# Hybrid encoder trunk: in the state-space groups, D times input moves to ScalarE, the masks come from the table of all heads, Y stands ahead of the last convolution, the scaling is shared and the chunk halves alternate

## The chip, the cores and the metric

The program runs on one core of one Trainium2 chip. The metric is device time in microseconds (us), the median of a few executions. TensorE (PE in the profile) multiplies matrices, VectorE (DVE), ScalarE (ACT) and GpSimd (POOL) do the elementwise work, and SyncE (SP) starts the loads of weights. The engines run side by side and wait for each other only by semaphores.

## The reference, cut to what matters

One layer over 512 frames and 1024 channels: a feed-forward part, a mixer of three branches (gated linear attention, a Mamba-2 state-space branch, chunked attention), another feed-forward part. The change touches the state-space branch alone:

```python
def _ssd(xh, bm, cm, dt, a):            # per chunk of 64 frames
        cum = jnp.cumsum(dac, axis=1)
        seg = cum[:, :, None] - cum[:, None, :]
        decay = jnp.exp(jnp.where(mask, seg, -jnp.inf))
        cb = jnp.einsum('btgn,bsgn->btsg', cc, bc)
        xdt = xc * dtc[..., None]
        y = jnp.einsum('btsg,btsgr,bsgrp->btgrp', cb, decay, xdt)
        y = y + jnp.einsum('btgn,bgrpn->btgrp', cc, state) * jnp.exp(cum)[..., None]
        to_end = jnp.exp(cum[:, -1:] - cum)
        state = jnp.exp(cum[:, -1])[..., None, None] * state + jnp.einsum('bsgn,bsgrp->bgrpn', bc, xdt * to_end[..., None])
...
    y = _ssd(xh, bm, cm, dt, a) + ssm_D.astype(F32).reshape(SSM_GROUPS, SSM_HPG)[..., None] * xh
    y = y.reshape(bsz, seq, SSM_D_INNER) * jax.nn.silu(z.astype(F32))
    y = _rmsnorm(y.reshape(bsz, seq, SSM_GROUPS, SSM_D_INNER // SSM_GROUPS), ...)
```

There are 8 groups of 4 heads of 64 channels, and 8 chunks of 64 frames. x, B and C come out of a projection, a causal convolution over 4 frames and a SiLU.

## The kernel before

Weights come from memory as 297 slabs of 128x1024, in the order of their use, into a ring of three buffers (RAW). ScalarE rounds each slab to WH (`hi`, L1025), VectorE subtracts to get the rest WL (`lo`, L1443), and TensorE multiplies WH by both parts of the activations and WL by one. So each slab costs three passes of eight matmuls (L534, and L576 for the z projection), and a slab must have been split before TensorE can use it. Every engine has its own program in a fixed order written by hand; the only thing that binds them is the semaphores.

The state-space groups take the time from about 427 us to 787 us. One pass of the loop (`ssm_round`) does two things at once: it projects and convolves the group p = i + 1, and carries out the chunked scan of the group `inner` = i, whose convolved x, B and C lie ready. In TensorE's order, a pass is:

- projection slab n (24 matmuls), then `ssm_turn`: twelve transposes of x into I01 and of B into I2, and the four `seg` matmuls (L677, L678) into I34, from the masked decay table MSH and its rest MSL
- slab n+1, then `ssm_cb_u`: the product C times B per chunk (L684), and seven state updates (L690, L695) from BK and XTE, whose results overwrite I01 and I34
- slabs n+2 and n+3, then `ssm_inter` (L712) and `ssm_intra` (L704: 32 small products of M and XDT, 64x64 each)
- the z projection of slabs n+4 and n+5 (L576, 96 matmuls), then `turn_back` (L721): eight transposes of Y.

Around it, ScalarE starts each convolution (L1109), copies I01 to XD (L1132) and I2 to BK, takes the exponential of I34 as M, the tanh of each convolution (L1120), the squares of Y (L1142), and evicts the turned Y (L1152). VectorE does the taps of the convolutions (L1626, three each), the SiLU products (L1645), XDT and XTE = XD times a factor for each head (L1665, L1667), the mask of CB, the chain of the states (13 steps), Y in four steps (L1705 to L1713), the variance (L1718), the scaling of Y (L1721), and MSH (L1609). GpSimd does MSL (L433), XD times D (L444) and the power -1/2 (L446). The first group has a prologue (`ssm_first`); the last one runs without a next group, beside the merge of this branch's output.

A few names: `gsc` is a copy of the 4 columns of a group out of SC, the table of all 32 heads. I01, I2, I34 and G are the banks of PSUM. Each matmul of f32 operands that isn't fp32r stands in the profile as two, so `ssm_intra` has 64 rows in the trace, and L684 has 16.

```python
                inc(nc.scalar.copy(XD[:].rearrange("p j c -> p (j c)"), I01[:]), "x_copied")
...
                x4 = XD[:].rearrange("p j (r c) -> p j r c", r=HPG)
                inc(nc.gpsimd.tensor_tensor(x4, x4, d, ALU.mult), "xd_ready")
```

Of the kernel before, what the change touches and what calls it, by code (L numbers as in the profile page):

```python
# [19 lines left out]
ALU = mybir.AluOpType  # L20
# [57 lines left out]
class At:  # L78
# [27 lines left out]
    def read(self):  # L106
# [9 lines left out]
        "ssm_squares": 4, "ssm_hi": 2,  # L116
# [5 lines left out]
        "m_ready": 1, "conv_done": 4, "ssm_chain": 13, "ssm_y": 4, "ssm_var": 1, "ssm_scaled": 4, "ssm_lo": 2,  # L122
# [4 lines left out]
    "gpsimd": {"da_lo_masked": 1, "xd_ready": 1, "ssm_rstd": 1, "gla_rstd": 1},  # L127
# [20 lines left out]
def build(nc, a, out):  # L148

    ctx = ExitStack()  # L150
    with ctx:
# [24 lines left out]
        minus_half = sb("minus_half", [P, TT])  # L176

# [176 lines left out]

        def over_tiles(ap):

            return ap.unsqueeze(1).to_broadcast([P, TT, HS])
# [39 lines left out]
        def _(pool):  # L397
# [11 lines left out]
            link(nc.gpsimd.memset(minus_half[:], -0.5))  # L409
            link(nc.gpsimd.memset(wgk_raw, 0.0))  # L410
# [18 lines left out]
            def da_lo(g):  # L429

                pool.wait_ge(sems["group_const"], after("group_const", g))
                pool.wait_ge(sems["intra_done"], last("intra_done", g - 1))
                inc(nc.gpsimd.tensor_tensor(MSL[:].rearrange("p (q t) -> p q t", t=CH),  # L433
                                            bc(gsc[:, 28:32, :].rearrange("p j r -> p (j r)"), CH),
                                            causal[:].unsqueeze(1).to_broadcast([P, TT * HPG, CH]), ALU.mult),
                    "da_lo_masked")

            def ssm(g):

                pool.wait_ge(sems["xte_ready"], after("xte_ready", g))  # L440
                pool.wait_ge(sems["group_norm"], after("group_norm", g))
                d = ggrp[:, 2:6].unsqueeze(1).unsqueeze(3).to_broadcast([P, TT, HPG, CH])
                x4 = XD[:].rearrange("p j (r c) -> p j r c", r=HPG)
                inc(nc.gpsimd.tensor_tensor(x4, x4, d, ALU.mult), "xd_ready")  # L444
# [54 lines left out]
            with pool.Fori(0, NG) as i:  # L499
                da_lo(i)  # L500
                ssm(i)

# [18 lines left out]
        def _(pe):  # L521
# [159 lines left out]
            def ssm_cb_u(g):  # L681
# [5 lines left out]
                pe.wait_ge(sems["xte_ready"], after("xte_ready", g))  # L687
                pe.wait_ge(sems["x_copied"], after("x_copied", g))
# [1472 lines left out]
```

## Time and profile before

| what | value |
|---|---|
| median of 3 executions | 1847.29 us (1846.70 to 1848.17) |
| the profiled execution's own time | 1847.36 us |
| its span in the trace | 1845.5 us |
| granted clock of TensorE, mean | 0.995 |
| busy: PE, DVE, ACT, POOL | 98%, 53%, 33%, 8% |

The profiled execution took what the others took, and its span leaves out 1.9 us at the ends. The busy share of PE counts every matmul from its start to its modelled end, and matmuls overlap; where TensorE really waits is seen from the idle time before its instructions, which the trace gives with the instruction that released them.

### The profile page before, as it was taken

The numbers are of one execution on the slowest core, as the hardware profiler recorded it, in microseconds if no ns is written. First come the engines' busy times: TensorE is split into PE (matmuls) and PEld (weight loads), VectorE is DVE, ScalarE is ACT, GpSimd is POOL, SyncE is SP. The second block draws the span as 40 slices with busy tenths as digits, with TensorE's granted clock in tenths as the row PEclk, the third lists the DMA queues.
The fourth block names the chain that finished last, engine by engine and source line by source line (L and its number), as shares of the span: only waits on it lengthen the run. The fifth ranks groups of instructions, "written<-read, shape, count | busy, mean of one in ns | idle before, by whom it ended". The sixth has DMA issues, their size and how long they took to land.

```text
span 1845.5 us, 26225 instructions
## 1 busy us (share of the span) xinstructions
PE 1806.9 (98%) x9852; PEld 1508.4 (82%) x9852; DVE 977.6 (53%) x1376; ACT 610.7 (33%) x942; POOL 145.1 (8%) x116
## 2 busy tenths in 40 slices
PE   7999999999999999999999999999999999999997
PEld 5888888878888888788988888887888888888885
DVE  6444443379888888732444445545334544444333
ACT  4323222233333344332233334443222422323221
POOL 4111100031111111100000000000000011111000
PEclk9999999999999999999999999999999999999998
DMA  4323223322222222132222222222222322223331
GB/s 154 103 93 100 93 101 103 110 84 70 73 74 69 68 68 68 58 103 91 92 69 82 90 87 82 84 78 89 95 99 91 103 92 92 101 92 101 103 105 66
DMA packets 47352, 164.91 MB, mean 89 GB/s; under 512 B 5520, under 2 KB 6672, under 8 KB 47296
## 3 DMA queue, kind: packets, MB, share of 16 engines
q1 hardware_dynamic: 43584, 158.10, 26.1%
q10 hardware_dynamic: 3712, 6.03, 1.0%
q8 instruction: 39, 0.64, 0.1%
q14 instruction: 17, 0.14, 0.0%
HBM read 162.01 MB, written 2.10 MB: 89 GB/s over the span
## 4 chain that ended last, share of the span: by engine, by line
PE 70%; issue 21%; DVE 6%; POOL 1%; ACT 1%; DMA 0%; DVEq 0%; POOLq 0%; ACTq 0%; SPq 0%
PE G L534 33%; PE G L576 12%; PE I L534 9%; PE G L550 7%; DVE WL L1443 2%; DVE CV L1626 1%; PE I L896 1%; POOL hid L456 1%; PE I L930 1%; PE I L906 1%; PE I L704 1%; PE I L712 1%; PE G L761 1%; DVE UL L1459 1%; DVE un L1581 1%
## 5 line engine op out<-in xcount | busy, mean ns | idle before, releaser
L1443 DVE TENSOR_TENSOR WL<-RAW,WH 128x1024 fp32r<-128x1024 f32 x297 | 387.9, 1309 | 298.2 <-ACT WH L1025 290.2
L1025 ACT CAST WH<-RAW 128x1024 fp32r<-128x1024 f32 x297 | 309.6, 1048 | 230.9 <-PE I L534 126.2
L534 PE MATMUL G<-UH,WH 128*128 128x512 f32 x696 | 172.8, 390 | 0.0
L534 PE MATMUL G<-UH,WL 128*128 128x512 f32 x696 | 171.9, 389 | 0.0
L534 PE MATMUL G<-UL,WH 128*128 128x512 f32 x696 | 171.9, 389 | 0.0
L534 PEld LDWEIGHTS G<-UH,WH 128*128 128x128 f32 x696 | 130.6, 188 | 28.0 <-issue 1.0
L534 PEld LDWEIGHTS G<-UH,WL 128*128 128x128 f32 x696 | 130.6, 188 | 27.1
L534 PEld LDWEIGHTS G<-UL,WH 128*128 128x128 f32 x696 | 130.6, 188 | 27.1
L534 PE MATMUL G<-NH,WH 128*128 128x512 f32 x448 | 113.2, 395 | 1.4 <-ACT SC L1098 1.4
L534 PE MATMUL G<-NL,WH 128*128 128x512 f32 x448 | 110.7, 389 | 0.0
L534 PE MATMUL G<-NH,WL 128*128 128x512 f32 x448 | 110.6, 389 | 0.0
L534 PEld LDWEIGHTS G<-NH,WH 128*128 128x128 f32 x448 | 82.4, 188 | 21.6 <-issue 5.1
L534 PEld LDWEIGHTS G<-NL,WH 128*128 128x128 f32 x448 | 84.1, 188 | 17.6
L534 PEld LDWEIGHTS G<-NH,WL 128*128 128x128 f32 x448 | 84.1, 188 | 17.5
L576 PE MATMUL G<-WH,NH 128*128 128x256 f32 x640 | 91.7, 286 | 3.6 <-DVE WL L1443 3.6
L576 PE MATMUL G<-WL,NH 128*128 128x256 f32 x640 | 91.0, 285 | 0.0
L576 PE MATMUL G<-WH,NL 128*128 128x256 f32 x640 | 90.7, 285 | 0.0
L456 POOL TENSOR_TENSOR hid<-hid,rms 128x512 f32<-128x512 f32 x44 | 57.3, 1302 | 397.8 <-ACT hid L1059 397.8
L576 PEld LDWEIGHTS G<-WH,NH 128*128 128x128 f32 x640 | 83.0, 192 | 6.2 <-issue 5.0
L534 PE MATMUL I<-HH,WH 128*128 128x512 f32 x352 | 87.6, 389 | 0.0
L534 PE MATMUL I<-HL,WH 128*128 128x512 f32 x352 | 87.6, 389 | 0.0
L534 PE MATMUL I<-HH,WL 128*128 128x512 f32 x352 | 87.6, 389 | 0.0
(299 smaller groups left out, 2477.5 us busy)
## 6 DMA issues: line engine op xcount, KB each, us to landing
RAW<-in_slabs SPq DMA_DIRECT2D x297, 512.0 KB, 3.3
h<-in_x SPq DMA_DIRECT2D x4, 512.0 KB, 6.8
bias<-in_rel ACTq DMA_DIRECT2D x16, 128.0 KB, 3.0
out_y<-h ACTq DMA_DIRECT2D x8, 256.0 KB, 2.2
bias<-in_rel ACTq DMA_DIRECT2D x16, 112.0 KB, 2.6
cst<-in_cst SPq DMA_DIRECT2D x1, 168.0 KB, 3.6
ut<-in_wgk SPq DMA_DIRECT2D x3, 32.0 KB, 8.8
```

The costliest lines, as they stand in the source:

```text
L456: nc.gpsimd.tensor_tensor(hid[:, t, :], hid[:, t, :], rms[:], ALU.mult).then_inc(gate_rms, 1)
L534: ins = mm(dst, W[:, n.slot, (k - k0) * P:(k - k0 + 1) * P], R[:, k, :], start=begin and which == 0 and k == k0, stop=end and which == 2 a ...
L550: ins = mm(dst, W[:, n.slot, k * P:(k + 1) * P], R[:, k, :], start=piece == 0 and k == 0, stop=piece == 5 and k == KT - 1)
L576: ins = mm(dst, U[:, k, j * P:(j + 1) * P], W[:, (n + k // 4).slot, (k % 4) * 256:(k % 4 + 1) * 256], start=which == 0 and k == 0, stop=wh ...
L704: ins = mm(I01[s, j * 256 + rr * CH:j * 256 + (rr + 1) * CH], M[s, j, rr, :], XDT[s, j, rr * CH:(rr + 1) * CH], start=True, stop=True)
L712: ins = mm(I34[half(c), (c // 2) * 256:(c // 2 + 1) * 256], CT[:, c * CH:(c + 1) * CH], SS[:, c, :], start=True, stop=True)
L761: ins = mm(G[:, wn.slot, :], W[:, n.slot, b * P:(b + 1) * P], R[:, k, :], start=begin and which == 0 and k == k0, stop=end and which == 2 ...
L896: ins = mm(head_psum(e, P_OFF[i], (i + 1) * P), AQ[par][s, f, i * P:(i + 1) * P], AK[par][s, f, 0:(i + 1) * P], start=True, stop=True)
L906: ins = nc.tensor.transpose(head_psum(e, PT_OFF[b] + (i - b) * P, P), PR[:, e, P_OFF[i] + b * P:P_OFF[i] + (b + 1) * P], ident[:])
L930: ins = mm(I01[half(e), b * P:T], AV[b // 2][:, b % 2, hd * CH:(hd + 1) * CH], src, start=b == 0, stop=b == TT - 1)
L1025: nc.scalar.copy(WH[:, n.slot, :], RAW[:, n.slot, :]).then_inc(split_hi, 1)
L1443: V.tensor_tensor(WL[:, n.slot, :], RAW[:, n.slot, :], WH[:, n.slot, :].bitcast(F32), ALU.subtract).then_inc(split_lo, 1)
```

## The change

Six edits, all in the state-space groups:

1. **D times input.** ScalarE no longer copies x as it is: four activations, one for each head, write XD = D times x straight from PSUM. GpSimd's product is gone. XTE and XDT are now made from I01 itself, XTE first, and TensorE's updates, which overwrite I01, wait for XDT too. The `hi` of slab n+3 moves behind the copies on ScalarE, the `lo` of slab n+3 behind XTE and XDT on VectorE.
2. **Masks.** MSH and MSL are made from SC instead of from `gsc`. MSH (`da_hi`) moves from the end of the pass to behind the last convolution, MSL (`da_lo`) to GpSimd's start of the pass before (it waits for the `intra` of the running group), and for group 0 right behind the split of the table.
3. **Y ahead of the last convolution** on VectorE: the four steps of Y stand behind the third SiLU, ahead of the fourth convolution's taps. ScalarE's squares stand ahead of the fourth tanh.
4. **Scaling.** The variance moves from VectorE to GpSimd, with the factor 1/256 folded into the squares. ScalarE scales two of the four tiles of Y, VectorE the two others.
5. **Order of `ssm_intra`:** the two 64-row halves alternate from product to product, where four products in one half were followed by four in the other.
6. One more constant (`four_eps`), set by GpSimd at the start.

```diff
             def ssm_intra():
-                for c in range(NCH):
-                    j, s = c // 2, half(c)
+                for j in range(TT):
                     for rr in range(HPG):
-                        ins = mm(I01[s, j * 256 + rr * CH:j * 256 + (rr + 1) * CH], M[s, j, rr, :],
-                                 XDT[s, j, rr * CH:(rr + 1) * CH], start=True, stop=True)
+                        for s in (half(0), half(1)):
+                            ins = mm(I01[s, j * 256 + rr * CH:j * 256 + (rr + 1) * CH], M[s, j, rr, :],
+                                     XDT[s, j, rr * CH:(rr + 1) * CH], start=True, stop=True)
@@ TensorE, ssm_cb_u
                 pe.wait_ge(sems["xte_ready"], after("xte_ready", g))
+                pe.wait_ge(sems["xdt_ready"], after("xdt_ready", g))
@@ GpSimd
             def da_lo(g):
-                pool.wait_ge(sems["group_const"], after("group_const", g))
                 pool.wait_ge(sems["intra_done"], last("intra_done", g - 1))
...
             def ssm(g):
-                inc(nc.gpsimd.tensor_tensor(x4, x4, d, ALU.mult), "xd_ready")
+                pool.wait_ge(sems["ssm_squares"], last("ssm_squares", g))
+                pool.wait_ge(sems["ssm_scaled"], last("ssm_scaled", g - 1))
+                pool.wait_ge(sems["ssm_scaled_act"], last("ssm_scaled_act", g - 1))
+                inc(nc.gpsimd.tensor_tensor(var4[:], ss4[:], four_eps[:], ALU.add), "ssm_var")
                 pool.wait_ge(sems["ssm_var"], after("ssm_var", g))
                 inc(nc.gpsimd.tensor_tensor(rstd4[:], var4[:], minus_half[:], ALU.pow), "ssm_rstd")
...
             da_split()
-            with pool.Fori(0, NG) as i:
-                da_lo(i)
+            pool.wait_ge(dt_pool, DA_SPLIT)
+            da_lo(0)
+            with pool.Fori(0, NG - 1) as i:
+                da_lo(i + 1)
                 ssm(i)
+            ssm(NG - 1)
@@ ScalarE
-                inc(nc.scalar.copy(XD[:].rearrange("p j c -> p (j c)"), I01[:]), "x_copied")
+                act.wait_ge(sems["group_norm"], after("group_norm", g))
+                for rr in range(HPG):
+                    ins = A(XD[:, :, rr * CH:(rr + 1) * CH],
+                            I01[:].rearrange("p (j c) -> p j c", j=TT)[:, :, rr * CH:(rr + 1) * CH], ACT.Copy,
+                            scale=ggrp[:, 2 + rr:3 + rr])
+                inc(ins, "x_copied")
...
+            def ssm_scale(g):
+                act.wait_ge(sems["ssm_rstd"], last("ssm_rstd", g))
+                for j in range(TT // 2):
+                    inc(A(Y[:, j, :], Y[:, j, :], ACT.Copy, scale=rstd4[:, j:j + 1]), "ssm_scaled_act")
@@ VectorE, one pass of the loop
                 for t in range(4):
                     conv_taps(p, t, n + t, wn + t)
-                    lo(n + t + 3)
                     if t == 0:
                         ssm_x(inner)
+                    lo(n + t + 3)
                     if t == 1:
                         ssm_m(inner)
                         ssm_chain(inner)
-                    if t == 3:
+                    conv_silu(p, t)
+                    if t == 2:
                         ssm_y(inner)
-                    conv_silu(p, t)
+                da_hi(p)
                 ssm_scale(inner)
```

**VectorE, the second half of a pass of the loop**, before (CV is a convolution's accumulator, BT and CT the convolved B and C of the next group, XD and ZS the factors and summands of Y):

```order
L1443 TENSOR_TENSOR WL<-RAW,WH 128x1024 [waits split_hi]
L1645 SCALAR_TENSOR_TENSOR BT<-TH,CV 128x512 [waits cb_done,conv_tanh]
L1624 REGISTER_ALU
L1626 SCALAR_TENSOR_TENSOR CV<-G,gconv,CV 128x511 [waits conv_begun]
...
L1443 TENSOR_TENSOR WL<-RAW,WH 128x1024 [waits split_hi]
L1705 TENSOR_TENSOR Y<-I,gsc 128x1024 [waits ssm_turned,inter_done]
...
L1711 TENSOR_TENSOR Y<-Y,XD 128x1024 [waits xd_ready,ssm_y]
...
L1645 SCALAR_TENSOR_TENSOR CT<-TH,CV 128x512 [waits inter_done,conv_tanh]
L1718 TENSOR_SCALAR var<-ss 128x4 [waits ssm_squares]
L1721 TENSOR_SCALAR Y<-Y,rstd 128x256 [waits ssm_rstd]
L1721 TENSOR_SCALAR Y<-Y,rstd 128x256 x3
```

and in the changed kernel, from the same place:

```order
L1465 TENSOR_TENSOR WL<-RAW,WH 128x1024 [waits split_hi]
L1669 SCALAR_TENSOR_TENSOR BT<-TH,CV 128x512 [waits cb_done,conv_tanh]
L1729 TENSOR_TENSOR Y<-I,gsc 128x1024 [waits ssm_turned,inter_done]
...
L1735 TENSOR_TENSOR Y<-Y,XD 128x1024 [waits x_copied,ssm_y]
...
L1650 SCALAR_TENSOR_TENSOR CV<-G,gconv,CV 128x511 [waits conv_begun]
...
L1465 TENSOR_TENSOR WL<-RAW,WH 128x1024 [waits split_hi]
L1669 SCALAR_TENSOR_TENSOR CT<-TH,CV 128x512 [waits inter_done,conv_tanh]
L1633 ISA [waits seg_done]
L1633 TENSOR_TENSOR MSH<-SC,causal 128x1024
L1743 TENSOR_SCALAR Y<-Y,rstd 128x256 [waits ssm_rstd]
L1743 TENSOR_SCALAR Y<-Y,rstd 128x256
```

The steps of Y have moved ahead of one convolution and one split; the mask MSH has come in between the last SiLU and the scaling, which has lost two of its four tiles and the variance.

**GpSimd, from the split of the table to the end of the loop**, before:

```order
L471 TENSOR_TENSOR SC<-SC,DAH 128x128
L499 UNCONDITIONAL_BRANCH
L499 ISA
L432 REGISTER_ALU [waits group_const]
L433 TENSOR_TENSOR MSL<-gsc,causal 128x1024 [waits intra_done]
L444 TENSOR_TENSOR XD<-XD,ggrp 128x1024 [waits group_norm,xte_ready]
L446 TENSOR_TENSOR rstd<-var,minus_half 128x4 [waits ssm_var]
```

and in the changed kernel:

```order
L472 TENSOR_TENSOR SC<-SC,DAH 128x128
L436 TENSOR_TENSOR MSL<-SC,causal 128x1024 [waits intra_done,dt_pool]
L502 UNCONDITIONAL_BRANCH
L502 ISA
L436 ISA [waits intra_done]
L436 TENSOR_TENSOR MSL<-SC,causal 128x1024
...
L443 ISA [waits ssm_squares]
L445 TENSOR_TENSOR var<-ss,four_eps 128x4 [waits ssm_scaled_act,ssm_scaled]
L447 TENSOR_TENSOR rstd<-var,minus_half 128x4 [waits ssm_var]
```

The first MSL now stands directly behind the split of the table, with no wait for VectorE; inside the loop MSL waits for the running group's `intra`, and the product for XD is gone.

**ScalarE, the start of a pass**, before:

```order
L1109 ACTIVATE CV<-G,gconv 128x512 [waits conv_done]
L1022 ISA
L1025 CAST WH<-RAW 128x1024 [waits slab_done,slab_landed0]
L1131 ISA [waits xb_turned]
L1132 COPY XD<-I 128x1024 [waits ssm_y]
L1133 REGISTER_ALU
L1134 COPY BK<-I 128x512 [waits u_done]
L1136 ACTIVATE M<-I 128x1024 [waits seg_done]
```

and in the changed kernel:

```order
L1115 ACTIVATE CV<-G,gconv 128x512 [waits conv_done]
L1137 ISA [waits xb_turned]
L1140 ACTIVATE XD<-I,ggrp 128x4x64 [waits group_norm,ssm_y]
L1140 ACTIVATE XD<-I,ggrp 128x4x64 x3
L1144 ISA
L1145 COPY BK<-I 128x512 [waits u_done]
L1028 ISA
L1031 CAST WH<-RAW 128x1024 [waits slab_done,slab_landed0]
L1149 ACTIVATE M<-I 128x1024 [waits seg_done]
```

The split of the slab has moved from ahead of the copies to behind them, and one copy has become four.

## Rows read from the trace of the kernel before

**Rows 1.** The page: each engine's busy time, share of the span, instructions.

```profile
PE 1806.9 (98%) x9852; PEld 1508.4 (82%) x9852; DVE 977.6 (53%) x1376; ACT 610.7 (33%) x942; POOL 145.1 (8%) x116
```

**Rows 2.** Waits of PE, 427 to 741 us: total, times, longest.

```profile
PE I L677 <- POOL MSL L433: 2.7, 6, 0.5
PE I L690 <- DVE XTE L1667: 2.3, 6, 0.4
```

**Rows 3.** Waits of PE, 741 to 792 us, the last group.

```profile
PE I L690 <- DVE XTE L1667: 2.3, 1, 2.3
PE I L721 <- DVE Y L1721: 0.8, 1, 0.8
PE I L712 <- DVE SS L1696: 0.3, 1, 0.3
```

**Rows 4.** Timeline of PE in one pass: start, length, [idle before <- releaser].

```profile
546.36 2.69 PE L704 MATMUL I<-XDT,M 64*64 64x64 f32 x64
548.98 1.22 PE L576 MATMUL G<-WH,NH 128*128 128x256 f32 x8
...
560.60 1.04 PE L721 MATMUL I<-ident,Y 128*128 128x128 f32 x8
...
568.88 0.49 PE L677 MATMUL I<-MSH,after_r 128*128 128x512 f32 x1 [0.44 <-POOL MSL L433]
...
575.45 0.69 PE L684 MATMUL I<-CT,BT 128*64 128x64 f32 x16
576.52 1.13 PE L690 MATMUL I<-XTE,BK 64*128 64x256 f32 x8 [0.39 <-DVE XTE L1667]
```

**Rows 5.** Groups of PE, 546 to 576.4 us: busy us, mean ns.

```profile
L704 PE MATMUL I<-XDT,M 64*64 64x64 f32 x64 | 2.7, 224 | 0.0
L684 PE MATMUL I<-CT,BT 128*64 128x64 f32 x16 | 0.7, 228 | 0.0
```

**Rows 6.** Timeline of DVE in the same pass.

```profile
547.26 2.31 DVE L1626 SCALAR_TENSOR_TENSOR CV<-G,gconv,CV 128x511 f32<-128x511 f32 x3
549.49 1.22 DVE L1443 TENSOR_TENSOR WL<-RAW,WH 128x1024 fp32r<-128x1024 f32 x1
...
553.13 1.23 DVE L1711 TENSOR_TENSOR Y<-Y,XD 128x1024 f32<-128x1024 f32 x1
...
559.26 1.14 DVE L1721 TENSOR_SCALAR Y<-Y,rstd 128x256 f32<-128x256 f32 x4 [1.12 <-POOL rstd L446]
...
565.65 1.23 DVE L1609 TENSOR_TENSOR MSH<-gsc,causal 128x1024 fp32r<-128x1024 f32 x1
566.79 2.92 DVE L1443 TENSOR_TENSOR WL<-RAW,WH 128x1024 fp32r<-128x1024 f32 x1
```

**Rows 7.** Timeline of ACT and POOL in the same pass.

```profile
562.79 1.28 ACT L1152 ACTIVATE SH<-I,ggrp 128x512 f32 x2
...
558.22 1.01 POOL L446 TENSOR_TENSOR rstd<-var,minus_half 128x4 f32<-128x4 f32 x1 [24.44 <-DVE var L1718]
565.86 2.78 POOL L433 TENSOR_TENSOR MSL<-gsc,causal 128x1024 fp32r<-128x1024 f32 x1 [6.63 <-DVE gsc L1605]
```

**Rows 8.** Timeline of the prologue: PE, DVE, ACT, POOL.

```profile
427.33 2.11 PE L534 MATMUL G<-NH,WH 128*128 128x512 f32 x8 [1.43 <-ACT SC L1098]
423.36 2.31 DVE L1626 SCALAR_TENSOR_TENSOR CV<-CT,gconv,CV 128x511 f32<-128x511 f32 x3
425.70 0.63 ACT L1120 ACTIVATE TH<-CV 128x512 f32<-128x512 f32 x1 [3.34 <-DVE CV L1626]
420.17 0.99 POOL L471 TENSOR_TENSOR SC<-SC,DAH 128x128 f32<-128x128 f32 x1
```

**Rows 9.** Windows: length, busy times, PEclk (the granted clock, 1.00 is 2.4 GHz).

```profile
753.49:755.30 1.81, 1.81 (x8) 1.53 (x10) 1.78 (x2) 0.00 (x0) 1.78 (x1) 0.50 0.57 233
```

**Rows 10.** Timeline of the last group: ACT and DVE.

```profile
748.92 1.02 ACT L1132 COPY XD<-I 128x1024 f32<-128x1024 f32 x1
752.23 1.21 DVE L1667 TENSOR_TENSOR XTE<-XD,gsc 128x1024 f32<-128x1024 f32 x1
```

More of the change, by code:

```diff
@@ L716, in turn_back @@
             def turn_back(src, dst, ready, g, done):
-                pe.wait_ge(sems[ready], last(ready, g))
+                for name in ready:
+                    pe.wait_ge(sems[name], last(name, g))
                 for f in range(2):
@@ L1110, in conv_begin @@
                       bias=gconv[:, 5 * t + 4:5 * t + 5], scale=gconv[:, 5 * t + 3:5 * t + 4]), "conv_begun")
-                if not raw:
+                if weights and not raw:
                     hi(n + 3)
@@ L1606, in group_scalars, with da_hi @@
                 dve.wait_ge(sems["group_const"], after("group_const", g))
-                dve.wait_ge(sems["intra_done"], last("intra_done", g - 1))
-                da = gsc[:, 24:28, :].rearrange("p j r -> p (j r)")
-                inc(V.tensor_tensor(MSH[:].rearrange("p (q t) -> p q t", t=CH), bc(da, CH),
-                                    causal[:].unsqueeze(1).to_broadcast([P, TT * HPG, CH]), ALU.mult), "da_hi_masked")
+            def da_hi(g):
+                dve.wait_ge(sems["seg_done"], after("seg_done", g - 1))
+                inc(V.tensor_tensor(MSH[:].rearrange("p (j r t) -> p j r t", j=TT, t=CH),
+                                    bc(SC[:, 24:28, bass.ds(HPG * g, HPG)], CH), causal_all, ALU.mult), "da_hi_masked")
             def group_norm(g):
@@ L1663, in ssm_x @@
                 dve.wait_ge(sems["x_copied"], after("x_copied", g))
+                inc(V.tensor_tensor(XTE[:].rearrange("p j (r c) -> p (j r) c", c=CH), heads(I01[:]), rows(2),
+                                    ALU.mult), "xte_ready")
                 dve.wait_ge(sems["intra_done"], last("intra_done", g - 1))
-                inc(V.tensor_tensor(XDT[:].rearrange("p j (r c) -> p (j r) c", c=CH), heads(XD[:].rearrange("p j c -> p (j c)")), rows(1),
+                inc(V.tensor_tensor(XDT[:].rearrange("p j (r c) -> p (j r) c", c=CH), heads(I01[:]), rows(1),
                                     ALU.mult), "xdt_ready")
-                inc(V.tensor_tensor(XTE[:].rearrange("p j (r c) -> p (j r) c", c=CH), heads(XD[:].rearrange("p j c -> p (j c)")), rows(2),
-                                    ALU.mult), "xte_ready")
             def ssm_m(g):
@@ L1709, in ssm_y @@
                 dve.wait_ge(sems["ssm_y"], after("ssm_y", g, 1))
-                dve.wait_ge(sems["xd_ready"], after("xd_ready", g))
+                dve.wait_ge(sems["x_copied"], after("x_copied", g))
                 inc(V.tensor_tensor(yf, yf, XD[:].rearrange("p j c -> p (j c)"), ALU.add), "ssm_y")
@@ L1715, in ssm_scale @@
             def ssm_scale(g):
-                dve.wait_ge(sems["ssm_squares"], last("ssm_squares", g))
-                inc(V.tensor_scalar(var4[:], ss4[:], 1.0 / 256, 4 * EPS, ALU.mult, ALU.add), "ssm_var")
                 dve.wait_ge(sems["ssm_rstd"], last("ssm_rstd", g))
-                for j in range(TT):
+                for j in range(TT // 2, TT):
                     inc(V.tensor_scalar(Y[:, j, :], Y[:, j, :], rstd4[:, j:j + 1], None, ALU.mult), "ssm_scaled")
```

50 lines of the change are left out of this document (27 added, 23 removed).

## The prediction

> **What bounds the kernel now.** First the page: TensorE is busy for 98% of the span, no other engine for more than 53% [rows 1], so work taken off another engine is worth only what TensorE has waited for it. The next view is therefore the waits of PE over the seven passes of the loop. Two lines matter: `seg` waited six times for GpSimd's MSL, 2.7 us in all, and the updates six times for VectorE's XTE, 2.3 us [rows 2]. In the timeline of one pass they are 0.44 us ahead of L677 and 0.39 us ahead of L690 [rows 4]. The last group, with no next group beside it, waited 2.3 us for XTE, 0.8 us for the scaled Y and 0.3 us for the chain of states [rows 3]. Nothing else in these stages held TensorE, except 1.43 us ahead of the first slab of the first pass, released by ScalarE's exponentials of the decay table; these stand behind the last tanh of the prologue (L1120 at 425.70), and that waited for the fourth convolution's taps, which VectorE did at 423.36 to 425.67 [rows 8]. The rest is TensorE's own pace. Behind the state-space groups TensorE is the bound too, so a us saved here comes out at the end.
>
> **Part 1, the order of `ssm_intra`.** The timeline has 64 half-products of 64 columns in 2.69 us, and 16 of 64 columns in 0.69 us for L684, whose outputs alternate between the two halves of the partitions [rows 4]. With the last one's own length taken off (224 and 228 ns, [rows 5]), that is (2.69 - 0.22) / 63 = 39 ns each against (0.69 - 0.23) / 15 = 31 ns. So neighbours in different halves already overlap more where they alternate one by one than where they alternate in fours. At 31 ns the 64 take 63 x 0.031 + 0.22 = 2.16 us, 0.53 us less; over 8 groups 4.2 us. Bounds: nothing, if the row half of the operands, which L684 doesn't split, changes the pace; and, if the two halves ran wholly side by side where now they did not at all, half of 2.69, 1.35 us a group, 10.8 us. I take the value of the nearest row.
>
> On the upper bound: TensorEngine Tiling (Array Packing) of the Trainium skill (Theoretical Speedup) gives up to 2x for operands of 64 by splitting the array into independent tiles. By it the change would save up to the bound just worked out; the rows show that a part of that overlap is there already.
>
> **Part 2, the masks.** MSL took GpSimd 2.78 us from 565.86, behind the copy of `gsc`, and came 0.44 us late [rows 7, 4]. Now it starts when `intra` ends, at about 549, a whole projection earlier, and MSH is made before the scaling. MSL is then ready 16 us ahead of `seg`, and MSH some 8. This ends the six waits: 2.7 us. While MSL ran, VectorE's split of a slab took 2.92 us instead of 1.22 [rows 6]: an operation with both inputs in SBUF loses 1.70 us beside MSL. That split stood ahead of the next pass's first taps, so its end frees VectorE 1.7 us sooner. GPSIMD Engine Reference of the Trainium skill (Key points) says that GpSimd shares SBUF interfaces with VectorE and contends with its instructions that have two SBUF inputs; by that rule, the trace agrees.
>
> The same 1.70 us must be paid elsewhere. In the loop it falls on Y (below). For group 0 MSL now starts behind the table's split, at 421.2 (420.17 + 0.99, [rows 8]), and VectorE is then in the third and fourth convolutions, reading SBUF on both sides, with no gap up to the fourth taps. These, the tanh and the exponentials, and so TensorE's first slab, all come 1.7 us later: **-1.7 us**. If the port were free (MSL between two operations) it would be nothing. TensorE then stands idle 1.43 + 1.7 = 3.1 us. In the last group, after a wait of 2.3 us [rows 3], its granted clock was 0.50 (1.2 GHz, half of full) for the next 1.81 us at least [rows 9]. A stretch at half speed loses half of itself, so that one cost 0.9 us or more. The bounds here are nothing and twice that row, 1.8; after the longer idle time I take **-1.5 us**, with a chance of about 6 in 10 that the clock falls at all.
>
> **Part 3, D on ScalarE.** The copy took 1.02 us [rows 10]. A scaled eviction of 512 columns takes 1.28 / 2 = 0.64 us [rows 7], so four of 256 columns lie between 4 x 0.32 = 1.3 and 4 x 0.64 = 2.6; I take 1.5, since a fixed part stays with each. (ScalarE: Activation LUTs of the Trainium skill, What ACT_TABLE_LOAD costs, would make it 4 x 0.4 = 1.6.) The slab's split, about 0.95 us, now stands behind them, so XD is ready 0.4 us sooner in a pass than now. VectorE does XTE and XDT, 1.15 us each, ahead of its own split. In a pass the updates had to wait until 576.5 [rows 4]. With the 1.7 us freed above and the split of 1.15 us out of the way, both products are done by about 573.5, 2 us and more ahead of TensorE: the six waits go, **2.3 us**. That cover is what hides the longer copies, and if it were gone, each 0.1 us late would cost 0.7 us.
>
> In the last group ScalarE's split stays ahead of the copies: XD runs 748.92 to 750.4, XTE and XDT end at about 752.85, and the updates start at 752.9 instead of 753.49: 0.6 us. The matrix M no longer meets GpSimd's product on VectorE, so the chain is on time: 0.3 us [rows 3]. The scaling is shared and saves 0.1 us or so. Together **1.0 us**.
>
> **Part 4, Y, scaling, variance.** No wait in the loop now: the turn started at 560.60, right at the end of the z projection, while VectorE's scaling ended at 559.26 + 1.14 = 560.40 [rows 4, 6]. Only 0.2 us spare, so this is what is late next. In the new order Y no longer waits behind taps and split (2.31 + 1.22 us, [rows 6]). Its second step waits for the end of `intra`, and then come: the rest of step 2, 1.2; MSL's hold, up to 1.7, in step 3 (Y<-Y,XD has both inputs in SBUF); steps 3 and 4, 2.5; taps, split and SiLU, 2.3 + 1.2 + 0.6; MSH 1.2; two scalings 0.6. Sum 11.3 us after `intra`. TensorE needs Y 560.60 - 548.98 = 11.6 us after `intra` [rows 4]. On ScalarE's side: Y's end at 5.4, squares 2.2, variance 0.2 to 1.0 (between nothing and a whole 1.01 us as the power takes, [rows 7]), the power 1.0, scaling 0.9: 9.7 to 10.5. So there are 0.3 us to spare on VectorE and 1 us on ScalarE: cost nothing, but thin. The new wait of TensorE on XDT is covered by part 3. The constant is set while GpSimd waits for its first input.
>
> **Sum.** 4.2 + 2.7 + 2.3 + 1.0 - 1.7 - 1.5 = 7.0 us. The profiled execution took 1847.36 us (its span and 1.9 us around it), 0.07 above the median: 1847.4 - 7.0 = **1840.4 us**. A measurement tells about 0.2%, 3.7 us, from no change.
>
> **Rivals.**
> - *The clock stays up*, at the start of the first pass and in the last group, whose wait is shorter by 0.6 us: 1.5 more, and up to 1.5 for the half speed seen at 753.49: 1837.4 to 1838.9. For it: after 1.43 us of idle time the first eight matmuls took 2.11 us, full pace [rows 8]. Chance 0.2.
> - *Full overlap in `intra`*: 10.8 instead of 4.2: 1833.8. Against it: the 39 ns are no sign that nothing overlaps now. Chance 0.04.
> - *`intra` doesn't change* (the change doesn't do there what it says): 4.2 less, 1844.6, within 0.2%. Speaks for it that no row has exactly this mixture of rows and columns at 64 columns. Chance 0.07.
> - *The turn becomes the wait*: the 0.3 us are used up by GpSimd's two small operations meeting VectorE, or by a longer hold. At 0.3 to 0.7 us over in each of 7 passes: 2 to 5 us lost, 1842.5 to 1845.5. Chance 0.13.
> - *Slower*: the same place, with MSL holding the port for its whole 2.78 us (1.1 more) and variance and power each waiting out an operation of VectorE of 1.2 us and holding it for their own 1.0 (2.0 more on VectorE): 3.1 - 0.3 = 2.8 us a pass, 19.6 us in seven, 1860.0. It decides from 1 us a pass on. Against it: MSL's neighbour lost 1.70, not 2.78. Chance 0.05.
> - The forecast as it stands: 0.51; its own range 1838.5 to 1842.5.
>
> **How the numbers follow.** Faster by over 0.2%: 0.51 + 0.20 + 0.04 and two thirds of the turn's wait, 0.09: 0.84. Same: 0.07 and 0.04: 0.11. Slower: 0.05. For the range I leave out slower and full overlap and the ends of the others: 1836.8 to 1844.6.
>
> **What would show it.** Right: the 64 rows of `intra` at about 2.15 us; no wait of L677's successor for MSL nor of the updates for XTE or XDT in the loop; the pass at 45.06 - 0.44 - 0.39 - 0.53 = 43.7 us; Y<-Y,XD near 2.9 us and the splits behind MSH at 1.2 us; the first slab's idle time near 3.1 us with VectorE's taps or split stretched in the prologue, and a half clock behind it; in the last group updates some 0.6 us earlier. Wrong: an idle time ahead of the turn in each pass, released by VectorE's or ScalarE's scaling; `intra` still at 2.69 us; the four copies over 2.6 us, which would bring the wait for XDT back.

## The result, and the profile after

The change made the kernel slower: a median of 1855.15 us in six executions (1853.24 to 1856.35), against 1847.18 us for the kernel before in as many; the ratio is 1.0041 (95% interval 1.0031 to 1.0052). That is 8 us more where 7 us less were forecast. The profiled execution took 1855.59 us, its span is 1853.9 us, and the mean granted clock is 0.995 as before.

The page of the changed kernel gives the first hint, in the row of busy times: TensorE does the same 9852 matmuls, but is busy for 1818.6 us, 11.7 us more than in [rows 1]. VectorE and GpSimd have less to do than before, as the change meant.

```profile
PE 1818.6 (98%) x9852; PEld 1500.2 (81%) x9852; DVE 963.4 (52%) x1352; ACT 621.2 (34%) x982; POOL 129.0 (7%) x117
```

So the second step is to find the stage. Each stage's length below is the time between the starts of two matmuls near its ends, the same two in every trace. The last two columns belong to experiments told further down: "no shift" is the change with one tile put elsewhere, "best" has one more edit.

| stage | before, us | after | no shift | best |
|---|---|---|---|---|
| first down projection (HH times weights) | 119.68 | +3.53 | 0.0 | 0.0 |
| prologue of the first group | 49.44 | +1.81 | +1.72 | 0.0 |
| seven passes of the loop | 314.30 | -7.02 | -8.17 | -11.05 |
| last group | 44.42 | -2.47 | -0.16 | -1.44 |
| merges and attention behind it | | +8.2 | 0.0 | 0.0 |
| second down projection | | +3.51 | 0.0 | 0.0 |

(The merges and attention are +2.47, +0.19, +0.71, +0.53 and +4.30 in their order.) The state-space groups, the only place that the change edits, are 7.7 us shorter with their prologue. Some 15 us are lost in stages where no line was edited. The loss can be seen in the timeline of PE at both ends of the first down projection. Before:

```profile
257.99 1.98 PE L534 MATMUL I<-HH,WH 128*128 128x512 f32 x8
259.80 1.98 PE L534 MATMUL I<-HL,WH 128*128 128x512 f32 x8
...
377.67 0.39 PE L561 MATMUL G<-UH,WH 128*128 128x512 f32 x1
```

And after:

```profile
258.27 2.03 PE L538 MATMUL I<-HH,WH 128*128 128x512 f32 x8
260.14 2.03 PE L538 MATMUL I<-HL,WH 128*128 128x512 f32 x8
...
381.47 0.40 PE L565 MATMUL G<-UH,WH 128*128 128x512 f32 x1
```

No row in between has an idle time. Eight matmuls start 1.81 us after the eight before them, and now 1.87 us: from matmul to matmul 226.7 ns before and 233.3 ns now (over the whole stage). Every one of the 528 is slower: each starts 230 to 236 ns after the one before it, where it was 226 or 227, although VectorE is busy for only 38% of the time between 270 and 370 us and ScalarE for 28%. A loss that came from meeting their work would spare the matmuls that don't meet it. The view of windows tells the same with a count. In a stretch of 100 us, with a granted clock of 1.00 (2.4 GHz) in both, the kernel before has 443 matmuls (first row), the changed one 430 (second):

```profile
270.00:370.00 100.00, 100.00 (x443) 1.00 0.32 105
```

```profile
270.00:370.00 100.00, 100.00 (x430) 1.00 0.31 100
```

The groups of PE in 40 to 250 us of the changed kernel show that the same kind of matmul with UH as the operand that streams keeps its mean of 389 ns:

```profile
L538 PE MATMUL G<-UH,WH 128*128 128x512 f32 x312 | 77.1, 389 | 0.0
```

while the groups of 262 to 376 us have 395 ns with HH, against 389 in the same group before (in each name pair the first operand streams through the array, the second is loaded as weights):

```profile
L538 PE MATMUL I<-HH,WH 128*128 128x512 f32 x161 | 41.1, 395 | 0.0
```

Over the two whole traces, some 3300 matmuls that stream 512 columns are slower by about 21 us in all. The 256-column ones, where WH streams and NH is loaded, are faster by 2.9 us in all; in the z projection they take 118.3 ns from start to start instead of 120.0.

Now the place of the change. The waits of PE in the seven passes have shrunk to one, of the prologue. None is left for MSL or XTE, and none has come at the turn [rows 2]:

```profile
PE G L538 <- ACT SC L1104: 3.3, 1, 3.3
```

The timeline of PE in one pass, which answers to [rows 4]:

```profile
535.42 0.69 PE L688 MATMUL I<-CT,BT 128*64 128x64 f32 x16
...
551.23 2.08 PE L709 MATMUL I<-XDT,M 64*64 64x64 f32 x64
553.24 1.21 PE L580 MATMUL G<-WH,NH 128*128 128x256 f32 x8
...
564.70 1.04 PE L727 MATMUL I<-ident,Y 128*128 128x128 f32 x8
...
572.41 0.48 PE L681 MATMUL I<-MSH,after_r 128*128 128x512 f32 x1
...
579.11 0.69 PE L688 MATMUL I<-CT,BT 128*64 128x64 f32 x16
```

`ssm_intra` takes 2.08 us instead of 2.69, and the pass 579.11 - 535.42 = 43.69 us instead of 45.06. That 43.7 was forecast is luck: without the slower pace the same pass takes 43.32 us (experiments 5 and 11), so the waits were worth more than the sum said, and the pace took that back. VectorE in the same pass [rows 6]:

```profile
551.68 1.22 DVE L1729 TENSOR_TENSOR Y<-I,gsc 128x1024 f32<-128x1024 f32 x1
553.42 1.22 DVE L1732 TENSOR_TENSOR Y<-Y,I 128x1024 f32<-128x1024 f32 x1 [0.53 <-PE I L709]
554.68 1.83 DVE L1735 TENSOR_TENSOR Y<-Y,XD 128x1024 f32<-128x1024 f32 x1
...
561.65 1.22 DVE L1633 TENSOR_TENSOR MSH<-SC,causal 128x1024 fp32r<-128x1024 f32 x1
562.78 0.60 DVE L1743 TENSOR_SCALAR Y<-Y,rstd 128x256 f32<-128x256 f32 x2
```

The second step of Y waits for the end of `intra`, as forecast; the third loses 0.6 us beside MSL, not 1.7. The scaling ends at 563.4, 1.3 us ahead of the turn. ScalarE and GpSimd [rows 7]:

```profile
572.83 1.57 ACT L1140 ACTIVATE XD<-I,ggrp 128x256 f32<-128x256 f32 x4 [0.51 <-PE I L674]
```

```profile
553.52 1.91 POOL L436 TENSOR_TENSOR MSL<-SC,causal 128x1024 fp32r<-128x1024 f32 x1 [34.61 <-PE I L709]
560.31 0.87 POOL L445 TENSOR_TENSOR var<-ss,four_eps 128x4 f32<-128x4 f32 x1 [4.88 <-ACT ssm_dump L1155]
561.26 1.33 POOL L447 TENSOR_TENSOR rstd<-var,minus_half 128x4 f32<-128x4 f32 x1
```

The four copies take 1.57 us (1.5 was forecast), and in the loop nobody waits for them. The prologue, PE and then DVE [rows 8]:

```profile
432.96 3.59 PE L538 MATMUL G<-NH,WH 128*128 128x512 f32 x8 [3.35 <-ACT SC L1104]
```

```profile
425.45 2.92 DVE L1465 TENSOR_TENSOR WL<-RAW,WH 128x1024 fp32r<-128x1024 f32 x1
428.89 2.31 DVE L1650 SCALAR_TENSOR_TENSOR CV<-CT,gconv,CV 128x511 f32<-128x511 f32 x3
```

It is the split, again at 2.92 us, that pays for GpSimd's first MSL. TensorE waits 3.35 us instead of 1.43, and its first eight matmuls then take 3.59 us instead of 2.11, with this granted clock in the window behind the wait (length, busy PE and its matmuls, PEclk, DMA share, GB/s):

```profile
433.00:439.00 6.00, 6.00 (x20) 0.73 0.05 6
```

So the local forecast held in its main terms, and the stages that are the same in both programs are what turned the sign. What can reach them is the one thing that the change leaves behind everywhere: the places of the tiles. `four_eps` is a tile of 16 B per partition, allocated right behind the small constant `minus_half`, and takes 32 B. By the addresses in the built programs, every later tile stands 32 B further on: HH from 120448 to 120480, NH from 108160, SL from 140928. The tiles allocated ahead of it have not moved: UH at 17536, where GH and SH lie too, WH at 62592, and WL. In the kernel before, the distance from WH to each of UH, NH, HH and SL is a multiple of 256 B (for HH 120448 - 62592 = 57856 = 226 x 256).

### The profile page after: what moved, and what is told of

The parts are those of the page before. It is cut to its first block, busy times and chain, and to the rows that moved or that the text cites. A ratio compares the mean times of both kernels' runs of the same rounds, so it can differ in the third digit from the quotient of the medians.

```text
span 1853.9 us, 26267 instructions
## 1 busy us (share of the span) xinstructions
PE 1818.6 (98%) x9852; PEld 1500.2 (81%) x9852; DVE 963.4 (52%) x1352; ACT 621.2 (34%) x982; POOL 129.0 (7%) x117
## 4 chain that ended last, share of the span: by engine, by line
PE 75%; issue 19%; DVE 4%; POOL 1%; ACT 0%; DMA 0%; POOLq 0%; DVEq 0%; SPq 0%; ACTq 0%
PE G L538 37%; PE G L580 12%; PE I L538 9%; PE G L554 7%; PE I L902 1%; POOL hid L457 1%; PE I L936 1%; PE I L912 1%; PE I L709 1%; PE I L717 1%; PE G L767 1%; DVE UL L1481 1%; PE I L727 1%; DVE CV L1650 1%; DVE un L1603 1%
## 5 line engine op out<-in xcount | busy, mean ns | idle before, releaser
L1465 DVE TENSOR_TENSOR WL<-RAW,WH 128x1024 fp32r<-128x1024 f32 x297 | 376.9, 1272 | 309.2 <-ACT WH L1031 300.4
L538 PE MATMUL G<-NH,WH 128*128 128x512 f32 x448 | 117.0, 403 | 3.3 <-ACT SC L1104 3.3
```

The costliest lines, as they stand in the source:

```text
L538: ins = mm(dst, W[:, n.slot, (k - k0) * P:(k - k0 + 1) * P], R[:, k, :], start=begin and which == 0 and k == k0, stop=end and which == 2 a ...
L1465: V.tensor_tensor(WL[:, n.slot, :], RAW[:, n.slot, :], WH[:, n.slot, :].bitcast(F32), ALU.subtract).then_inc(split_lo, 1)
```

## The experiments

Each has 4 to 11 executions, and ratios are to the kernel before, timed beside it on the same chip. Experiments 1 to 4, 5 to 8 and 9 to 12 had a chip each; the median of the kernel before was 1847.1, 1847.6 and 1847.5 us on them, so differences between experiments hold to about 0.5 us.

**1. The change with an unused tile of 32 B behind `four_eps`.** The shift is then 64 B.

```diff
         four_eps = sb("four_eps", [P, TT])
+        sb("spare", [P, TT])
```

> The changed kernel with a second tile of 128x4 behind four_eps, which nothing uses: it moves every later SBUF tile by another 32 B. In the built program four_eps had moved them from addresses that 64 divides to addresses with a remainder of 32; the spare tile brings the remainder back to 0. Theory A (the new constant's place slows TensorE): matmuls that stream a tile behind it (HH, NH, NL, SL, AH, MH) went from 226.7 to 233.3 ns each, 3247 of them, 21.5 us, and the 256-column ones gained 2.9: the time falls by about 18.6 us to 1836.6, and the first down projection is 119.7 us again, not 123.2. Rival B (the instruction stream, its length or place in memory, sets the pace): nothing moves, 1855. Rival C (the new order of GpSimd and VectorE loads SBUF more): nothing moves either.

Measured: 1841.41 us (1837.92 to 1841.89), ratio 0.9964 (0.9951 to 0.9978): a tile that no instruction touches makes the changed kernel 13.7 us faster. The pace of the down projection is 228.9 ns from start to start, between the two others, with 438 matmuls in the window. The pace gained more than the medians tell, since TensorE was at half speed for longer here (mean granted clock 0.992 in four of the five executions, 0.993 to 0.996 in the changed kernel's). The window:

```profile
270.00:370.00 100.00, 100.00 (x438) 1.00 0.32 104
```

**2. The kernel before with the unused tile, and nothing else.**

```diff
         minus_half = sb("minus_half", [P, TT])
+        sb("spare", [P, TT])
         LR = ...
```

> The kernel before with a spare tile of 128x4 in the place where the change put four_eps, and no other edit: later tiles move by 32 B. Theory A: about 18 us slower, 1865, with the pace of the down projection at 233 ns and that of the feed-forward's first part (UH, UL, in front of it) still at 227. Rivals B and C: no change, 1847.2.

Measured: 1864.02 us (1863.71 to 1864.20), ratio 1.0090 (1.0075 to 1.0106), 16.9 us slower. The group of 262 to 376 us has the changed kernel's 395 ns; in the first feed-forward stage it is still 389:

```profile
L535 PE MATMUL I<-HH,WH 128*128 128x512 f32 x163 | 41.8, 395 | 0.0
```

```profile
L535 PE MATMUL G<-UL,WH 128*128 128x512 f32 x312 | 77.1, 389 | 0.0
```

No instruction differs between this kernel and the one before. The shift alone does the damage, and none of the edits to the engines' orders is needed for it.

One more thing shows in this trace, in the merges. SH, WH and WL lie ahead of the spare tile, so none of them has moved, and yet some blocks of SH are slow:

```profile
816.96 2.03 PE L535 MATMUL G<-NH,WL 128*128 128x512 f32 x8
818.82 2.01 PE L535 MATMUL G<-SH,WH 128*128 128x512 f32 x8
820.67 2.03 PE L535 MATMUL G<-SL,WH 128*128 128x512 f32 x8
822.54 2.01 PE L535 MATMUL G<-SH,WL 128*128 128x512 f32 x8
824.39 1.98 PE L535 MATMUL G<-SH,WH 128*128 128x512 f32 x8
826.21 2.03 PE L535 MATMUL G<-SL,WH 128*128 128x512 f32 x8
```

The blocks of SH that stand directly behind a block of a moved tile (NH, SL) take 1.85 us, the one behind another block of SH takes 1.82; in the kernel before all take 1.81 to 1.82. So the operands of the matmul itself are not the whole of it: what the blocks before it streamed counts as well.

**3. The kernel before with the new order of `ssm_intra` alone** (part 5 of the change, and no new tile).

> The kernel before with the order of ssm_intra alone changed (halves alternate). The term of the forecast: 0.53 us a group; the changed kernel's trace has 2.08 us instead of 2.69, 0.61 a group, so 4.9 us over eight: 1842.3. Rival: what intra gives up is taken again by the wait for the scaled Y (only 0.2 us spare there), then 0.2 to 0.4 us a pass remain, 1844 to 1845.5. No address changes.

Measured: 1842.69 us (1841.98 to 1844.48), ratio 0.9975 (0.9965 to 0.9985), 4.4 us faster. The waits of PE in the seven passes:

```profile
PE I L690 <- DVE XTE L1667: 2.2, 6, 0.4
PE I L721 <- DVE Y L1721: 1.7, 6, 0.3
```

The saving in `intra` is made, and 1.7 us come back at the turn, where VectorE's scaling had 0.2 us to spare before. The wait for MSL no longer shows as an idle time, but it is not all gone: `seg` starts 0.57 us after the transposes of B ahead of it, 1.04 us in the kernel before and 0.36 us where it has nothing to wait for (experiment 5).

**4. As 1, and the first MSL waits for VectorE's `group_const`** (it then meets no split in the prologue).

```diff
             pool.wait_ge(dt_pool, DA_SPLIT)
+            pool.wait_ge(sems["group_const"], after("group_const", 0))
             da_lo(0)
```

> The kernel of e1 in which the first MSL waits for the copy of the group's scalars again, as before the change, and so runs after the prologue's convolutions. Forecast of this term: the 1.7 us on the wait of the first slab (1.43 before, 3.3 after) and the half-speed stretch behind it (1.5 us) come back: 3.2 us below e1. Rival: the clock falls anyway or the first pass's seg waits for MSL: 0 to 1.9 us.

Measured: 1836.42 us (1835.72 to 1838.60), ratio 0.9946 (0.9932 to 0.9959), 5.0 us below experiment 1. PE waits 1.9 us ahead of its first slab instead of 3.8, and the prologue is as long as in the kernel before. Not all of the 5.0 us need belong to this edit: of the 5.1 us between the two profiled executions 2.6 lie in the last group, where TensorE was at half speed for 6.8 us in experiment 1 and not at all here, and the edit touches nothing there.

**5. As 4, with `four_eps` in spare columns of a tile that exists:** no tile moves.

```diff
-        four_eps = sb("four_eps", [P, TT])
-        sb("spare", [P, TT])
...
-        gconv = sb("gconv", [P, 20])
+        gconv_all = sb("gconv", [P, 24])
+        gconv, four_eps = gconv_all[:, 0:20], gconv_all[:, 20:24]
```

> The kernel of e4 with the new constant in four spare columns of another tile (gconv, whose 80 B take up 96), so that no tile moves at all against the kernel before. If a tile's address sets the pace, the 512-column matmuls on HH and NH are back at 226.7 ns (e1 and e4, moved by 64 B: 228.9) and the 256-column ones at 120 (e4: 116.7); from e4's trace outside the state-space stage that nets 1.5 us less: 1835. Rival (e1 helped for another reason than addresses): no change from 1836.4.

Measured: 1836.22 us (1834.19 to 1837.42), ratio 0.9935 (0.9921 to 0.9948). This is the fastest of all, 11.4 us under the kernel before. Every stage outside the state-space groups has the length of before (last column of the table), and the window has its 443 matmuls again.

A pass is 43.32 us, from two turns in the timeline of PE:

```profile
556.60 1.04 PE L728 MATMUL I<-ident,Y 128*128 128x128 f32 x8
...
599.91 1.04 PE L728 MATMUL I<-ident,Y 128*128 128x128 f32 x8
```

**6 and 7. As 4, with larger shifts:** `four_eps` as in the change, and an unused tile of 64 B (shift 96 B) or 96 B (shift 128 B) behind it.

> The kernel of e4 with a longer spare tile: everything behind it moves by 96 B, a remainder of 32 by 64. Theory A1 (only the remainder by 64 counts, odd multiples of 32 B are slow): 233.3 ns in the down projection, 1854. Theory A2 (each distance has its own pace, since 64 B gave 228.9 and not 226.7): something else, between 226.7 and 233.3, 1835 to 1854.

> The kernel of e4 with everything moved by 128 B. If the pattern repeats after 128 B, it is the kernel of f1: 226.7 and 120 ns, 1835. If it repeats after 64 B only roughly, or not at all within 128: 228.9 as in e4 or another pace.

Measured: 1854.20 us (1852.32 to 1856.70), ratio 1.0032 (1.0020 to 1.0044), and 1852.88 us (1851.05 to 1856.46), ratio 1.0030 (1.0019 to 1.0041). These are 18.0 and 16.7 us over experiment 5, from which they differ in addresses alone. Both have 233.3 ns in the down projection; the group of 262 to 376 us in the one of 128 B:

```profile
L540 PE MATMUL I<-HH,WH 128*128 128x512 f32 x162 | 41.5, 395 | 0.0
```

So it is no matter of 64 B lines alone: 64 B is nearly free, 128 B is not.

**8. As 5, with the old order of `ssm_intra`.**

```diff
-                for j in range(TT):
+                for c in range(NCH):
+                    j, s = c // 2, half(c)
                     for rr in range(HPG):
-                        for s in (half(0), half(1)):
...
```

> The kernel of f1 with the old order of ssm_intra (four products in one half, then four in the other). Forecast: 0.61 us in each of 8 groups more, f1 plus 4.9, 1840. Rival: a part less, if the wait for the scaled Y takes it: then the same edit is worth less beside the other edits than alone (it gave 4.4 us alone).

Measured: 1840.56 us (1840.13 to 1841.31), ratio 0.9960 (0.9946 to 0.9973), 4.3 us over experiment 5. The group of `intra` in the seven passes, as in the kernel before (first row, from this experiment) and with the alternating order (second row, from experiment 5):

```profile
L710 PE MATMUL I<-XDT,M 64*64 64x64 f32 x448 | 18.8, 224 | 0.0
```

```profile
L710 PE MATMUL I<-XDT,M 64*64 64x64 f32 x448 | 14.6, 220 | 0.0
```

**9. The kernel before with 32 B ahead of its very first tile:** all tiles move, UH, WH, HH and NH alike.

> The kernel before with a spare tile of 32 B ahead of the very first tile: the streamed operands (UH, HH, NH and so on) and the slabs (WH, WL) all move by 32 B, so their distances stay. If the distance between the two operands of a matmul sets the pace, nothing changes: 1847.2, 226.7 ns in every stage. If each operand's own address does, the first feed-forward stage is slowed as well, and the time goes beyond the 1864 of e2, to about 1875 to 1880.

Measured: 1847.78 us (1846.74 to 1850.16), ratio 1.0003 (0.9994 to 1.0012): no change, and 389 ns in both stages:

```profile
L535 PE MATMUL I<-HH,WH 128*128 128x512 f32 x168 | 41.8, 389 | 0.0
```

HH stands at 120480 here, exactly where it stands in the changed kernel with its 395 ns. It isn't the address of a tile by itself, then, but where it lies against the tiles that stand ahead of it.

**10. The kernel before with its later tiles moved by 256 B.**

```diff
         minus_half = sb("minus_half", [P, TT])
+        sb("spare", [P, 64])
...
-        rc = sb("rc", [P, 2, TT], F32, w)
+        rc = gconv[:, 0:2 * TT].rearrange("p (e i) -> p e i", e=2)
```

> The kernel before with all tiles from LR on moved by 256 B (to make room, the small tile rc of the attention stage, 32 B, lies in the dead tile gconv). Moves of 32, 96 and 128 B gave 233.3 ns in the down projection, 64 B 228.9. If the pattern repeats after 256 B: 1847.2 and 226.7 ns. If not: 1850 to 1865.

Measured: 1848.42 us (1846.78 to 1851.35), ratio 1.0005 (0.9996 to 1.0014), at 226.7 ns. A move of 256 B is as good as none.

**11. The change whole, with `four_eps` in the spare columns** (as in 5, and the first MSL where the change has it). This is the change as the forecast took it, without its shift.

> The changed kernel whole, with the new constant in four spare columns of the tile gconv, so that no tile moves against the kernel before. This is the change as the forecast took it. Forecast 1840.4. From the runs: f1 (1836.2) plus the price of the early first MSL, 1.9 us of wait (3.8 against 1.9 in the profiles of e1 and e4) and a stretch at half speed behind it: 1839.5 to 1841.

Measured: 1837.92 us (1836.76 to 1842.18), ratio 0.9948 (0.9934 to 0.9961), 17.2 us under the changed kernel. The profiled execution is the slowest of the five, 1842.18 us; its windows behind the wait in the prologue, which is 3.1 us long here, show TensorE at half clock for about 6.8 us (columns: length, busy PE, PEld, DVE, ACT, POOL, then PEclk, DMA share, GB/s):

```profile
429.00:432.00 3.00, 1.93 (x5) 1.55 (x6) 2.80 (x5) 2.85 (x9) 0.00 (x0) 0.58 0.00 0
432.00:435.00 3.00, 3.00 (x9) 2.32 (x8) 2.97 (x6) 0.85 (x1) 0.00 (x0) 0.50 0.00 0
435.00:438.00 3.00, 3.00 (x12) 2.41 (x11) 1.35 (x3) 0.00 (x0) 0.00 (x0) 0.79 0.59 187
```

It had a second such stretch in the last group (746.9 to 753.7 us). The mean granted clock fits: 0.992 in this execution, 0.994 or 0.995 in the four others. It is the likely reason why this execution is slower than they are, and why the "no shift" column of the table is short of the best one by 2.9 and 1.3 us.

**12. As 5, with Y back behind the fourth convolution's taps.**

```diff
-                    conv_silu(p, t)
-                    if t == 2:
+                    if t == 3:
                         ssm_y(inner)
+                    conv_silu(p, t)
```

> The kernel of f1 with the four steps of Y back behind the fourth convolution's taps and split. Forecast part 4: the move of Y pays for the pass becoming shorter. Without it the turn waits: in e3 it waited 0.28 us a pass with intra 0.6 us shorter; here the MSL beside Y and the mask MSH ahead of the scaling come on top, so 1 to 2 us a pass, 7 to 14 us in all, 1843 to 1850. Rival: VectorE's earlier start of the pass covers it, 1836 to 1839.

Measured: 1848.82 us (1847.28 to 1851.32), ratio 1.0008 (0.9999 to 1.0017), 12.6 us over experiment 5. The waits of PE in the seven passes, the turn of one pass, and what VectorE does ahead of it:

```profile
PE I L728 <- DVE Y L1744: 10.1, 6, 1.7
```

```profile
561.50 1.09 PE L728 MATMUL I<-ident,Y 128*128 128x128 f32 x8 [1.68 <-DVE Y L1744]
```

```profile
555.00 1.23 DVE L1738 TENSOR_TENSOR Y<-Y,ZS 128x1024 f32<-128x1024 f32 x1
559.09 0.69 DVE L1670 SCALAR_TENSOR_TENSOR CT<-TH,CV 128x512 f32<-128x512 f32 x1 [2.87 <-ACT TH L1127]
559.70 1.21 DVE L1634 TENSOR_TENSOR MSH<-SC,causal 128x1024 fp32r<-128x1024 f32 x1
560.84 0.60 DVE L1744 TENSOR_SCALAR Y<-Y,rstd 128x256 f32<-128x256 f32 x2
```

Y is done at 556.2, ScalarE's squares and, behind them, the fourth tanh follow, VectorE waits 2.87 us for that tanh, and then the SiLU and MSH stand ahead of the scaling. So nothing of the gain is left. This holds for ScalarE's order as the change has it, with the squares ahead of the tanh: the wait of 2.87 us for that tanh comes from setting only one of the two engines back. The old order of both was not tried with the new masks, so 12.6 us is the price of this mixture and not shown to be that of Y's place alone.

## Why the prediction was wrong, step by step

**The step that failed** is the last sentence of part 4: "The constant is set while GpSimd waits for its first input." It priced the instruction, which is indeed free, and not the tile. The tile's 32 B cost 17.2 us (changed kernel against experiment 11) and 16.9 us in the kernel before (experiment 2). The forecast had no term and no rival for it, and its slower rival had another place and mechanism. The bound "TensorE's own pace" was taken as fixed; in these runs it hangs on where the operands lie. Experiments 1, 2, 5, 6 and 7 show it for tiles moved against the ones ahead of them, experiment 9 that the address by itself does nothing, experiment 10 that 256 B more does nothing. Nothing moves one operand alone against all other tiles, and the blocks of SH in experiment 2 show that the pair of operands of a matmul is not the whole rule.

**The rest of the sum**, 7.0 us, is to be held against experiment 11, which gained 9.6 us in the median (1837.92 us for a forecast of 1840.4, inside the range given, with terms that missed both ways):

- *Part 1, 4.2 us.* Right in kind and slightly small: 0.60 us a group instead of 0.53 (18.8 - 14.6 = 4.2 us over seven groups), 4.8 us for eight. Done alone it brought 4.4, and in the last place 4.3. The upper bound from full overlap was far off.
- *Parts 2 and 3, six waits each, 2.7 and 2.3 us.* All gone, but worth more than their idle time. A pass became 45.06 - 43.32 = 1.74 us shorter in experiment 5, while `intra` and both idle times make 0.60 + 0.44 + 0.39 = 1.43. The starts of the matmuls around the two waits show the other 0.3 us. First the four transposes of B, from which `seg` started 568.88 - 567.84 = 1.04 us later in the kernel before (first row), and 0.36 us later in experiment 5:

```profile
567.84 0.60 PE L670 MATMUL I<-ident,BT 128*128 128x128 f32 x4
```

```profile
563.83 0.60 PE L675 MATMUL I<-ident,BT 128*128 128x128 f32 x4
564.19 0.48 PE L682 MATMUL I<-MSH,after_r 128*128 128x512 f32 x1
```

  That is 0.68 us for an idle time of 0.44. Between the product C times B and the updates it was 1.07 us [rows 4] and became 0.62: 0.45 us for an idle time of 0.39. Without a wait the next matmul starts before the modelled end of the one ahead of it, and the idle time leaves that overlap out. Over six passes it is 1.9 us that the sum didn't have.
- *Part 3, last group, 1.0 us.* Experiment 5 gained 1.44 us there with `intra`'s 0.6, so 0.8. The updates started 0.5 us sooner in the group (0.6 forecast), but by another path than was thought: the longer copies for XD hold up the copy BK behind them, and TensorE now waits 1.4 us for BK ahead of the product C times B (0.3 before, a wait that the forecast left out) and 1.3 us ahead of the updates instead of 2.3. The clock blurs the rest: the group gained 0.2 us in experiment 11, with half speed for 6.8 us, 1.4 in experiment 5, with half speed for a stretch (0.78 between 739 and 745 us), and 2.5 in the changed kernel, at full speed and in spite of the slower pace.
- *The first MSL, -1.7 us.* Right: the split was stretched from 1.22 to 2.92 us, TensorE's idle time grew to 3.35 us (3.1 forecast), and the prologue was 1.72 us longer in experiment 11. Experiment 4 took the term away.
- *The clock, -1.5 us at 6 in 10.* Behind the longer wait it fell to 0.50 (1.2 GHz) in all three traces that have it from this cause (the changed kernel, experiments 1 and 11). Behind the 1.9 us of experiment 4 (0.72 between 427 and 433 us) and the 3.0 us of experiment 6 it fell too, behind the 1.4 us of experiment 5 it stayed at 1.00. In the changed kernel the window from 433 us has 0.73 over 6 us, so 3.2 us at half speed and 1.6 lost; in experiment 11 some 6.8 us at half speed, 6.2 of them behind the wait, and 3.1 lost. As the best execution of experiment 11 lies within 0.6 us of the median of experiment 5, it can't have fallen as far in all. The size varies from execution to execution.
- *Part 4, nothing.* Right, with more room than was thought: 1.3 us on VectorE instead of 0.3. MSL cost Y<-Y,XD 0.6 us where 1.7 was taken from the split, since MSL started when the second step did and ran 1.91 us, more than half of it beside that step, which reads PSUM. What Y<-Y,XD lost is about what was left of MSL. GPSIMD Engine Reference of the Trainium skill (Key points) speaks of contention for instructions with two inputs in SBUF; the trace agrees, as the second step, with one input in PSUM, kept its 1.22 us beside MSL. GpSimd's variance and power took 0.87 and 1.33 us, together 0.2 more than the upper bounds; ScalarE waited 1.97 us for the result, TensorE did not. Experiment 12 shows that this step protects something, but not how much, as it sets only VectorE's order back.

The rival *the turn becomes the wait* did not come; in experiment 3, with `intra` alone and Y where it was, it did, by 0.3 us a pass. *Full overlap* and *`intra` unchanged* are excluded by the 14.6 us. *The clock stays up* was true of the prologue of experiment 5, not of the change.

## What to carry to other kernels

A new tile is an edit to every tile behind it: note the addresses of the operands of the hot matmuls before and after a change, keep the distances as they were where the pace was good (here multiples of 256 B; put small constants behind the large tiles, or into spare columns), and compare matmuls' pace in stages that the change doesn't touch before explaining any loss in the stage that it does. In a trace an idle time between pipelined matmuls understates what a wait costs, by the overlap that it breaks. An agreement in one number, as the 43.7 us here, can be two errors that cancel: take the unwanted part out and look again. A step that gains nothing alone can carry others, so undo each part from the whole change as well as doing it alone, on every engine that it touches.

## What the runs showed of the hardware

**Matmul pace and the place of the operands in SBUF.** Start to start at a granted clock of 1.00, for a stream of 512 columns of HH against WH in the down projection, and for 256 columns of WH against NH in the z projections, by how much HH and NH were moved against WH (from a multiple of 256 B):

| moved by | 512 columns | 256 columns | experiments |
|---|---|---|---|
| 0, or both moved | 226.7 ns | 120.0 ns | before, 5, 9, 11 |
| 32 B | 233.3 | 118.3 to 118.4 | after, 2 |
| 64 B | 228.9 | 117.8 | 1, 4 |
| 96 B | 233.3 | 117.4 | 6 |
| 128 B | 233.3 | 118.6 | 7 |
| 256 B | 226.7 | 120.0 | 10 |

The long streams lose up to 2.9%, the short ones gain up to 2.2% (at 64 B 114.8 ns, 4% less, in the projections of the two branches behind). UH against WH, neither of them moved, kept its 226.7 ns in all; the sixteen products of the states with C, both of them moved, kept their 1.88 us. SH and GH against WH or WL, none of them moved, took 232 ns at 32 B in all 25 blocks of eight from 786 us on that stand directly behind a block of a moved tile, and 227 ns in all 19 others (both in the changed kernel and in experiment 2). Moves of 160 to 224 B were not tried. What the distance does inside the chip stays open: the traces show a slower stream with no idle time and no longer loads of weights (188 ns before, 187 in experiment 2), and nothing of the reads themselves.

**GpSimd and VectorE.** The same mask on GpSimd takes 1.91 to 2.78 us by its neighbours; a split of VectorE beside it 2.92 us instead of 1.22, but Y<-Y,XD 1.83 instead of 1.23. In every one of the eight pairs of the kernel before and the eight of the changed one, the operation of VectorE ends 1.08 us after the mask does, however long the two stood side by side: the split in the prologue 428.37 - 427.29, Y<-Y,XD 556.51 - 555.42, the split of [rows 6] 569.72 - 568.64. An undisturbed operation of this size ends 1.13 us after the one ahead of it. So it looks as if VectorE's operation did not begin before the mask was done, and its loss is what is left of the mask when it comes up. A sum of 4 elements a partition took GpSimd 0.87 us in the loop, where it ended 0.06 us after the split that ran beside it, and 0.20 us in the last group.
